# The finest score level of a gated linear attention: pair products on VectorE and one matmul with ones, in place of eight chunk matmuls

## What is computed

```
bc = jnp.cumsum(to_chunks(log_a), axis=-2)
diff = b_[..., :, None, :] - b_[..., None, :, :]
decay = jnp.exp(jnp.where(causal, diff, -jnp.inf))
attn = jnp.einsum('bhik,bhjk,bhijk->bhij', q_, k_, decay)
o = jnp.einsum('bhij,bhjv->bhiv', attn, v_) + jnp.einsum('bhik,bhkv->bhiv', q_ * jnp.exp(b_), state)
```

## Time and profile before

| what | value |
|---|---|
| median of 3 runs | 2337.24 us (2336.74 to 2341.07) |
| the profiled execution | 2339.24 us, of which the span is 2337.4 us |
| TensorE busy | 2309.3 us, 99% of the span, granted clock 0.998 |
| VectorE busy | 1565.5 us, 67% |
| ScalarE busy | 844.8 us, 36% |
| GpSimd busy | 776.9 us, 33% |

### The profile page before, as it was taken

The page is one execution under the profiler, slowest core; times in us unless marked ns, Lnnn a source line. Parts: engine busy times, 40 slices in busy tenths (PEclk is TensorE's granted clock), DMA queues, the critical chain, the costliest instruction groups (busy, mean ns, idle before and its releaser), DMA issues. The chain is left out here.

```text
span 2337.4 us, 30876 instructions
## 1 busy us (share of the span) xinstructions
PE 2309.3 (99%) x10848; PEld 1914.9 (82%) x10848; DVE 1565.5 (67%) x1981; ACT 844.8 (36%) x1223; POOL 776.9 (33%) x525
## 2 busy tenths in 40 slices
PE   8999999999999999999999999999999999999998
PEld 5788888888879888888888887788888888888887
DVE  8856665677745885784785694742686666667677
ACT  5333333343664234224224232421443333333443
POOL 3454545100432223212213235213455454550002
PEclk9999999999999999999999999999999999999999
DMA  5233333557832022122123136444323333327566
GB/s 155 97 106 110 92 112 90 190 178 228 284 100 60 28 91 64 37 89 75 28 73 100 36 118 208 140 146 137 124 78 92 112 90 112 90 94 260 164 222 232
DMA packets 238750, 282.92 MB, mean 121 GB/s; under 512 B 11184, under 2 KB 164272, under 8 KB 235824
## 3 DMA queue, kind: packets, MB, share of 16 engines
q1 hardware_dynamic: 232112, 268.89, 36.5%
q10 hardware_dynamic: 6528, 12.58, 1.4%
HBM read 208.56 MB, written 72.88 MB: 120 GB/s over the span
## 5 line engine op out<-in xcount | busy, mean ns | idle before, releaser
L714 PE MATMUL PU<-XH,w_h 128*128 128x512 f32 x992 | 393.6, 397 | 7.0 <-DVE gt L2517 3.5
L716 PE MATMUL PU<-XH,w_l 128*128 128x512 f32 x992 | 386.9, 390 | 0.0
L715 PE MATMUL PU<-XL,w_h 128*128 128x512 f32 x992 | 386.6, 390 | 0.0
L2620 POOL TENSOR_TENSOR ws<-pw,ws 128x512 fp32r<-128x512 f32 x168 | 244.2, 1456 | 221.5 <-ACT ws L1364 191.4
L2360 DVE SCALAR_TENSOR_TENSOR PG<-ub,cw,PG 128x512 f32<-128x512 f32 x464 | 308.1, 751 | 5.9 <-issue 5.9
L2615 POOL TENSOR_TENSOR w_l<-w_raw,w_h 128x2048 fp32r<-128x2048 f32 (+1 forms) x39 | 174.9, 4484 | 313.3 <-ACT w_h L1267 313.3
L714 PEld LDWEIGHTS PU<-XH,w_h 128*128 128x128 f32 x992 | 186.7, 188 | 50.0 <-POOL w_l L2615 7.0
L2620 POOL TENSOR_TENSOR ws<-s_sum,ws 128x512 fp32r<-128x512 f32 x122 | 159.6, 1316 | 179.3 <-ACT ws L1364 179.3
L716 PEld LDWEIGHTS PU<-XH,w_l 128*128 128x128 f32 x992 | 186.5, 188 | 39.5
L715 PEld LDWEIGHTS PU<-XL,w_h 128*128 128x128 f32 x992 | 186.8, 188 | 37.8 <-issue 0.2
L2091 DVE TENSOR_TENSOR f_l<-f_raw,f_h 128x1024 fp32r<-128x1024 f32 x110 | 136.8, 1249 | 58.1 <-ACT f_h L1543 58.0
(11 more groups left out here) (412 smaller groups left out, 5358.4 us busy)
## 6 DMA issues: line engine op xcount, KB each, us to landing
pw<-in_ffn_w_in SPq DMA_DIRECT2D x86, 512.0 KB, 5.7
f_raw<-f_d SPq DMA_DIRECT2D x154, 256.0 KB, 3.1
f_raw<-in_ffn_w_out SPq DMA_DIRECT2D x132, 256.0 KB, 4.1
w_raw<-in_w_mix_in SPq DMA_DIRECT2D x50, 512.0 KB, 4.7
f_d<-s_buf SPq DMA_DIRECT2D x22, 1024.0 KB, 5.0
f_d<-hid SPq DMA_DIRECT2D x21, 512.0 KB, 2.6
x_d<-FACC SPq DMA_DIRECT2D x16, 512.0 KB, 3.3
gate_d<-tmp ACTq DMA_DIRECT2D x16, 512.0 KB, 2.8
```

Of the source, the lines that this page charges most:

```text
L714: pe.matmul(dst, hi(k), xh(k), start=(n == 0), stop=False)
L715: pe.matmul(dst, hi(k), xl(k), start=False, stop=False)
L716: last = pe.matmul(dst, lo(k), xh(k), start=False, stop=(n == KT - 1))
L2620: PT(ws[:, i, 1, :, :], form_source(name, par), ws[:, i, 0, :, :], ALU.subtract).then_inc(form_lo, 1)
```

## The change

Level 0 pairs each odd token (query) with the even one ahead of it (key), so it has 512 scores a head. The change computes each of them directly. `minus(1)` makes one difference for a pair, b of the odd token less b of the even one, 512 in all and packed into the first half of R[:, 1, :]. The exponential covers these 512. `times(1)` multiplies by the query of the odd token and then, after a semaphore wait on its own first step, by the key of the even one. `level(0)` sums over the features with a single matmul: a 128 x 128 tile of ones as stationary operand, the 512 products as moving one. All 128 rows of the result hold the same sums, and `select(0)` picks from them with the mask as before. The tile of ones is new (64 KB in all, in a place that is free during the heads) and is filled once on VectorE in the first head's prologue, which gives a third count to `gla_zero`.

```diff
+        ones_f = at("ones_f", 203.5, [P, P])
...
+        pair_half = sem("pair_half")
...
                     pe.wait_ge(t_ready, 8 * h + m + 1)
+                    if lv == 0:
+                        pe.wait_ge(gla_zero, 3)
+                        pe.matmul(GL[:, 0:HALF], ones_f[:, :], R[:, m, 0:HALF], start=True, stop=True).then_inc(g_done, 1)
+                        return
                     for c in range(TT):
...
                         act.wait_ge(d_ready, 8 * h + m + 1)
-                        A(R[:, m % 3, :], R[:, m % 3, :], ACT.Exp, scale=1.0 / 16).then_inc(e_ready, 1)
+                        r = R[:, 1, 0:HALF] if m == 1 else R[:, m % 3, :]
+                        A(r, r, ACT.Exp, scale=1.0 / 16).then_inc(e_ready, 1)
...
             dve.memset(S_sb[:, 0, :], 0.0).then_inc(gla_zero, 1)
+            dve.memset(ones_f[:, :], 1.0).then_inc(gla_zero, 1)
...
+                    if m == 1:
+                        TT_(r[:, 0:HALF].rearrange("p (s n) -> p s n", n=1), bv[:, :, 1, :], bv[:, :, 0, :], ALU.subtract)\
+                            .then_inc(d_ready, 1)
+                        return
                     mid = bv[:, :, 0, n - 1:n].to_broadcast([P, SEQ // (2 * n), n])
...
+                    if m == 1:
+                        pairs = r[:, 0:HALF].rearrange("p (s n) -> p s n", n=1)
+                        TT_(pairs, pairs, qv[:, :, 1, :], ALU.mult).then_inc(pair_half, 1)
+                        dve.wait_ge(pair_half, h + 1)
+                        TT_(pairs, pairs, kv[:, :, 0, :], ALU.mult).then_inc(t_ready, 1)
+                        return
```

## The result

The changed kernel is slower: 2341.30 us against 2337.45 us as medians of 22 runs each, ratio 1.0016 with an interval of 1.0010 to 1.0022. (One execution of the changed kernel took 5961 us, in a disturbed state, and is left out of the interval.) Forecast were 2333.7 us and a ratio of 0.9985. The profiled execution took 2339.97 us with a span of 2338.2.

A forecast was written before the change was run, and what follows sets the result against it. The prediction took TensorE's issue time to bound the heads. Saving 0.89 us in each of four heads, 3.56 us, with other engines priced at 0, turned 2337.24 into 2333.7 us; range 2330.9 to 2337.2.

The forecast's parts named there:

- the sum for a head: TensorE at level 0: eight multiplies of 1.75 us replaced by one of 0.86, saving 0.89 us a head.
- nothing is added at the seams: TensorE around level 0: level 1's first load lies under the new multiply's stream, so no extra time.
- 181.48 us from head to head, busy throughout: Sign for the heads: 181.48 us between level 0 starts instead of 182.37, with TensorE never idle.
- (e): Rival: VectorE meets GpSimd's long subtraction twice a head, TensorE waits 2.1 us at level 3; 2342.3 us, chance 0.06.
- The new multiply: Level 0 on TensorE: one ones multiply over 512 columns, two records of 0.43 us, 0.86 us in all.
- Rival (d): Columns, not weight loads, set a small multiply's price at level 0, so hardly any saving: 2336.9 us, chance 0.04.
- VectorE: VectorE's work for level 0: net -0.5 us a head, off TensorE's path, so priced at 0.
- the 0.12 of the forecast: VectorE's product for m = 1: its second instruction waits for the first, adding 0.12 us.
- The long wait beside GpSimd: VectorE's 5.10 us subtraction moves from m = 4 to the first for m = 5, about 748.0 to 751.5; price 0.
- Behind the heads: After the heads, the chains of waits move with TensorE, so the saving is kept and waits stay unchanged.
- (b): Rival: saving lost behind the heads as waits grow by up to 3.56 us; 2335.3 to 2337.2 us, chance 0.10.
- rival (c): Waits behind the heads shrink by at least 1.2 of 6 us; 2330.5 to 2332.5 us, chance 0.10.

The follow-up runs named there:

- e1: Changed kernel plus 28 idle TensorE instructions in head 0, putting the loop's start back where it was before the change: 2333.76 us, ratio 0.9983 to the kernel before.
- e2: Kernel before, with head 0's level 0 cut to one of eight multiplies, moving the loop's start as the change does: 2342.68 us, ratio 1.0022.
- e3: Changed kernel with TensorE's loop over heads 1 to 3 written out, so without a jump: 2334.90 us, ratio 0.9989 to the kernel before.
- e7: Kernel before with only the change's VectorE and ScalarE part; TensorE keeps its eight level 0 multiplies: 2337.69 us against 2338.16, ratio 0.9999.
- e6: Changed kernel plus 236 idle TensorE instructions in head 0, 20 short of a full block of 256: 2340.46 us, one execution.
- e5: Changed kernel plus 8 idle TensorE instructions in head 0: 2333.33 us, one execution.

## Why the prediction was wrong, point by point

**The step that failed** is the sum for a head, with its sentence that "nothing is added at the seams", and with it the view that TensorE's queue inside the heads is worth its matmuls alone. I priced what each of TensorE's instructions takes to run. I gave no price to the place of the code, and the change takes 28 instructions from the code ahead of a loop. The seams that I looked at were those between matmuls; the one that mattered was the jump from the loop's end to its start. e1, e2 and e3 together show it: the position alone brings the loss (e2), the change without the position doesn't (e1), nor the change without the jump (e3). Of the signs that the prediction gave, "181.48 us from head to head, busy throughout" is the one that failed, for two of three heads. None of the rivals named the cause. (e) foresaw "slower" by another mechanism, VectorE late for level 3, and that did not happen.

**The new multiply** was right in its mechanism: 0.86 us as forecast, saving 0.94 and in the windows 0.95 us a head in place of 0.89. The term was mis-sized by 0.06, since I had given each of two levels half of 3.50; level 1 by itself takes 1.70. Rival (d), by which small multiplies cost their columns alone, would have had a saving of some 0.1 us a head; it is excluded. The forecast time of 2333.7 is nearly what e1 measured (2333.76), but that it agrees to 0.1 is luck: the saving was 3.98 us instead of 3.56, and the kernel before stood at 2337.74 beside e1 instead of 2337.24.

**VectorE** did as forecast. The timeline of the changed kernel in head 0, which answers to the earlier trace rows:

```profile
722.29 0.69 DVE L2415 TENSOR_TENSOR R<-R,q_sb 128x512 f32<-128x512 f32 x1
723.01 0.69 DVE L2417 TENSOR_TENSOR R<-R,k_sb 128x512 f32<-128x512 f32 x1
...
742.38 1.32 DVE L2435 COPY_PREDICATED A_sb<-masks,PG 128x512 f32<-128x512 uint8 x1 [8.29 <-issue]
743.50 0.71 DVE L2401 TENSOR_TENSOR R<-b_sb 128x512 f32<-128x512 f32 x1
744.13 0.68 DVE L2402 TENSOR_TENSOR R<-b_sb 128x512 f32<-128x512 f32 x1
744.73 1.34 DVE L2435 COPY_PREDICATED A_sb<-masks,PG 128x512 f32<-128x512 uint8 x1
745.86 3.98 DVE L2401 TENSOR_TENSOR R<-b_sb 128x512 f32<-128x512 f32 x1
```

The second product starts 0.72 us after the first and not 0.60, the 0.12 of the forecast. The long wait beside GpSimd (now 4.93 us from 744.36) has moved from the second subtraction for m = 4 to the first for m = 5, as forecast, and is 3.98 us instead of 5.10 (the forecast had 3.5). Nothing on TensorE waits for it, and e7 puts VectorE's part at 0.

**Behind the heads** the saving is kept, so (b) did not happen. In e1 TensorE waits 2.7 us for GpSimd's weight rest and 2.4 for VectorE, against 2.77 and 3.11 in the earlier trace rows, and the wait of 0.43 is gone, about 1 us less in all. That looks like rival (c) in small, but it can't be put down to the new multiply: e7, where TensorE does the work of before, has 2.8 and 2.5 and no third wait, and e3, with the whole change, has 2.8 and 2.9. These are single executions, and the cause is open.

**What I could have read.** The page of the kernel before shows 66 instruction transfers on a queue of their own, and its trace shows VectorE standing twice for 3.0 us for issue, in its loop over the same heads, at 1039.17 and 1221.53, shortly behind the ends of heads 1 and 2, where it cost TensorE nothing:

```profile
DVE PG L2360 <- issue: 5.9, 2, 3.0
```

That VectorE's waits have the same cause was not tried. But the sign was there that a jump back can cost 3 us; I had not asked what it would take for TensorE's to do so.

The Trainium skill describes the mechanism (Runtime: NRT & Kernel Launch, section Instruction fetch mechanics): code comes in blocks of 16 KiB, 256 instructions, fetched in order, and a taken branch whose target isn't at hand forces a fetch. The two more blocks of 16 KB for two jumps and the distance of 256 in e6 agree. What cost time here is not the target's own block, though: in the changed kernel its transfer begins at 1030.28, ahead of the pass's first matmul at 1032.91, and what TensorE waits for is the block behind it.

## What to carry to other kernels

When an engine that sets the time runs a loop, adding or taking away instructions ahead of the loop can cost time in each pass, whatever the instructions do (here 3 to 5 us). After each such edit look in the engine's waits for a line that ends in "issue" and in the timeline for a gap just behind the loop's first instructions. If it is there, move the loop's start by a few idle instructions, or write the loop out; both took the waits away here. And before a small edit is judged by its time, it should be measured in both positions; here the edit is worth -3.7 us and its position +7.5.

The version to use is e1: 0.17% faster than the kernel before, and 0.3% faster than the changed one.

## What the runs showed of the hardware that was not expected

- TensorE waits 2.4 to 3.0 us on the loop's first instructions when the block's border comes within the first seven (changed kernel and e2). When some 26 instructions with 11 matmuls stand ahead of it, the pass loses 0.7 us (e6). It doesn't wait at all when the loop begins just behind a border (e5) or 20 further (e1). Where the borders lie is worked out from the waits.
- After three of four waits of 2.4 to 3.0 us the granted clock was 0.50 for about 3 us, at 1.6 us each; after one it stayed at 1.00, and so it did after the short waits of e6. What decides between them was not tried.
- The transfers of code themselves are short. In the changed kernel those around the first jump were, on q8 (start and duration in us, from the trace's DMA records; each 16 KB)

```
1030.28  0.94
1033.84  1.05
1039.61  1.35
```

The transfer that begins at 1033.84 ends at 1034.88, and TensorE goes on at 1036.38. It is the transfer's start, 3.56 us after the one before it, that is late, and 1.5 us pass after its end. The same order holds at all six waits of the changed kernel, e2 and e6: TensorE goes on 1.2 to 1.5 us after the second block has landed. The spacing is not the change's doing: at the first jump it is 3.61 us in the kernel before, 3.59 in e1 and 3.80 in e5, where nearly a whole block of work covers it. At the second jump it is 3.26 us in the changed kernel and 3.10 in e2, and there the waits are shorter too (2.69 and 2.44). Why the second block is asked for only then is open; it was not tried.
- Idle instructions on TensorE are nearly free where matmuls are long: from head 0's gate logits to its level 0 there are 48.48 us with none (changed kernel), 48.49 with 8 and 48.48 with 28, one behind each group of three matmuls, and 50.55 with 236, three behind each group.
